# A two-block network on one core: routing rearranged, and the last layer's first expert group selected by TensorE

## The reference

```python
mix = jnp.concatenate([o_dn, o_sa.astype(o_dn.dtype)], axis=-1) @ w_out[l]
h = layer_norm(DEEPNORM_ALPHA * h + mix, ln1_g[l], ln1_b[l])
ffn = hier_moe(h, w_grp[l], b_grp[l], w_rtr[l], b_rtr[l], w1[l], w3[l], w2[l])
h = layer_norm(DEEPNORM_ALPHA * h + ffn, ln2_g[l], ln2_b[l])
...
    grp_prob = jax.nn.softmax((t @ w_grp).astype(F32) + b_grp, axis=-1)
    g_prob, g_sel = lax.top_k(grp_prob, 1)
...
    e_prob, e_sel = lax.top_k(jax.nn.softmax(in_grp, axis=-1), TOP_K_IN_GROUP)
...
    hid = jax.nn.silu(jnp.einsum('td,edf->tef', t, w1)) * jnp.einsum('td,edf->tef', t, w3)
    y = jnp.einsum('tef,efd->td', hid * combine[..., None].astype(hid.dtype), w2)
```

## Time and profile before

| | us |
|---|---|
| three executions | 1302.36, 1304.57, 1306.28 (median 1304.57) |
| profiled execution, its own time | 1303.69 |
| its span, first to last instruction | 1301.9 |
| TensorE busy | 1261.1 (97%) |
| VectorE / ScalarE / GpSimd busy | 573.9 / 485.3 / 115.3 |
| read from HBM | 301.06 MB |

### The profile page before, as it was taken

The page is one execution under the profiler, slowest core; times in us unless marked ns, Lnnn a source line. Parts: engine busy times, 40 slices in busy tenths (PEclk is TensorE's granted clock), DMA queues, the critical chain, the costliest instruction groups (busy, mean ns, idle before and its releaser), DMA issues.

```text
span 1301.9 us, 19435 instructions
## 1 busy us (share of the span) xinstructions
PE 1261.1 (97%) x7553; PEld 811.2 (62%) x7553; DVE 573.9 (44%) x1280; ACT 485.3 (37%) x1064; POOL 115.3 (9%) x167
## 2 busy tenths in 40 slices
PE   8999999999999999999999998999999989999996
PEld 7888588885787877554444433778877544344432
DVE  3335223262676585462222225677585443222224
ACT  3346343462753245212223233663235313223232
POOL 0000000000014321000000000004322000000000
PEclk9999999999999999999999999999999999999999
DMA  9753162332521124759999999221133769999994
GB/s 367 151 179 108 54 269 97 130 106 77 211 98 67 66 97 166 286 219 394 420 420 422 421 415 385 104 98 66 66 130 119 317 237 397 421 421 422 422 421 177
DMA packets 48847, 307.40 MB, mean 236 GB/s; under 512 B 5897, under 2 KB 6409, under 8 KB 16752
## 3 DMA queue, kind: packets, MB, share of 16 engines
q1 hardware_dynamic: 43760, 288.61, 56.3%
q0 software_dynamic: 3200, 8.16, 2.8%
q10 hardware_dynamic: 1792, 9.32, 1.9%
HBM read 301.06 MB, written 8.59 MB: 238 GB/s over the span
## 4 chain that ended last, share of the span: by engine, by line
PE 79%; DVE 13%; ACT 5%; issue 2%; DMA 1%; ACTq 0%; DVEq 0%; SPq 0%; POOLq 0%
PE ps L1151 22%; PE ps L1878 18%; PE ps L1905 9%; PE ps L1191 4%; PE ps L1455 4%; PE ps L1947 2%; PE ps L1968 2%; PE ps L1119 2%; DVE projT L2829 1%; DVE small L2828 1%; PE ps L1693 1%; PE ps L1887 1%; PE ps L1929 1%; DVE projT L2820 1%; PE ps L1584 1%
## 5 line engine op out<-in xcount | busy, mean ns | idle before, releaser
L1151 PE MATMUL ps<-hT,ring 128*128 128x272 f32 (+1 forms) x1760 | 416.8, 390 | 0.6 <-ACT hT L2065 0.6
L1151 PEld LDWEIGHTS ps<-hT,ring 128*128 128x128 f32 x1760 | 327.1, 190 | 62.7 <-issue 7.7
L1878 PE MATMUL ps<-ring,arena 128*64 128x512 f32 x416 | 138.6, 598 | 0.0
L3273 DVE TENSOR_TENSOR xo<-ps,xo 128x512 fp32r<-128x512 f32 x64 | 42.9, 689 | 99.6 <-ACT xo L2502 99.4
L3394 POOL TENSOR_TENSOR arena<-projT,cst 32x272 f32<-32x272 f32 x104 | 71.5, 688 | 114.2 <-DVE projT L2807 101.1
L1878 PE MATMUL ps<-projT,arena 128*64 128x512 f32 x240 | 80.0, 597 | 0.9 <-issue 0.9
L3264 DVE TENSOR_TENSOR arena<-arena,ps 128x256 f32<-128x256 f32 x32 | 13.5, 421 | 141.4 <-ACT arena L2489 140.8
L1878 PEld LDWEIGHTS ps<-ring,arena 128*64 128x64 f32 x416 | 40.2, 137 | 51.9 <-issue 51.1
L2487 ACT ACTIVATE arena<-ps 128x256 f32<-128x256 f32 x32 | 12.3, 383 | 138.0 <-PE ps L1878 138.0
L1455 PE MATMUL ps<-ring,projT 128*128 128x512 f32 x128 | 57.0, 598 | 0.0
L1191 PE MATMUL ps<-ring,arena 128*128 128x512 f32 x128 | 55.9, 593 | 0.0
(11 more groups left out here) (526 smaller groups left out, 2056.9 us busy)
## 6 DMA issues: line engine op xcount, KB each, us to landing
ring<-experts SPq DMA_DIRECT2D x72, 1024.0 KB, 16.5
ring<-w_in SPq DMA_DIRECT2D x62, 1024.0 KB, 5.6
projT<-experts SPq DMA_DIRECT2D x48, 1024.0 KB, 15.9
arena<-experts SPq DMA_DIRECT2D x22, 1024.0 KB, 12.6
prm<-experts SPq DMA_DIRECT2D x22, 1024.0 KB, 16.0
ring<-w_out SPq DMA_DIRECT2D x16, 1024.0 KB, 5.0
spare<-experts SPq DMA_DIRECT2D x12, 1024.0 KB, 14.6
lent<-experts SPq DMA_DIRECT2D x8, 1024.0 KB, 10.2
```

The lines of the kernel that those rows point to most:

```text
L1151: mm = pe.matmul(ps[:, chunk_bank(blk, l, j), 0:ncols], w[:, j % 2, k, :], hT[:, k, T - ncols:T], start=(k == 0), stop=(k == KC - 1))
L1878: mm = pe.matmul(ps[64 * e:64 * e + 64, 0, :], xg[:, 4 * h + k, i % 2, 64 * e:64 * e + 64], w[e][:, k // 2, 512 * (k % 2):512 * (k % 2) + ...
L3273: v.tensor_tensor(low, ps[:, 4 + half, :], high, ALU.subtract).then_inc(s("pair_rows_copied"), 1)
```

## The change

In both layers: tile 0's logits use 16 stationary columns and bank 0 (`logits_of`) in place of 128 columns and a copy; every tile's logits raise `logits_done`, and VectorE takes the tiles one by one; the four operations behind ScalarE's exponentials move behind the first pair selection; two fillers grow. In the last layer: `router_turn` and the logits of tile 1 move one step back in the out projection; TensorE selects the first group's rows itself from `res`, in two halves (`first_rows`); ScalarE copies them into `xrows`; the row numbers come later, from the places; GpSimd, SP, TensorE, VectorE and ScalarE no longer use a fetch for group 0. The stores of the normed rows stay, since groups 1 to 3 are still fetched.

```diff
+        def fetched(l, g):
+            return 16 * (GROUPS * l + g + 1 - (l == LAYERS - 1))
...
                         sp.wait_ge(layer_normed, normed_at[l, 1, 2, 1])
-                        sp.wait_ge(rows_fetched, 16 * (GROUPS * l + 1))
+                        if l < LAYERS - 1:
+                            sp.wait_ge(rows_fetched, fetched(l, 0))
...
+        def logits_of(t):
+            return ps[0:ROWS[t], 1 if t else 0, 64 * t:64 * t + 36]
...
-                        mm = pe.matmul(ps[:, 1, 64 * t:64 * t + 36], h2T[:, k, COL[t]:COL[t] + P], wr[:, k, :],
+                        mm = pe.matmul(logits_of(t), h2T[:, k, COL[t]:COL[t] + ROWS[t]], wr[:, k, :],
                                        start=(k == 0), stop=(k == KC - 1))
-                    if t != 1 or l == LAYERS - 1:
-                        mm.then_inc(s("logits_done"), 1)
+                    mm.then_inc(s("logits_done"), 1)
...
-                    if t == (0 if l < LAYERS - 1 else 2):
+                    if t == 0:
                         router_turn(0, 1)
...
                         if t == 2 and i == 0:
                             if l < LAYERS - 1:
                                 router_turn(1, 0)
-                            router_sums_made()
-                            router_logits(0, 1)
-                        if t == 2 and i == 1 and l < LAYERS - 1:
-                            router_logits(1, 0)
+                                router_sums_made()
+                                router_logits(0, 1)
+                            else:
+                                router_turn(0, 1)
+                        if t == 2 and i == 1:
+                            if l < LAYERS - 1:
+                                router_logits(1, 0)
+                            else:
+                                router_sums_made()
+                                router_logits(0, 1)
...
+                def first_rows(half):
+                    pe.wait_ge(s("group_selected"), 1)
+                    for t in tiles:
+                        mm = pe.matmul(ps[:, 2 + half, :], xsel[:, t, :], res[:, t, 512 * half:512 * half + 512],
+                                       start=(t == t0), stop=(t == 2))
+                    mm.then_inc(s("group_rows_done"), 1)
...
-                first_tokens()
-                keep_busy(5, 512, 512)
+                if l < LAYERS - 1:
+                    first_tokens()
+                    keep_busy(5, 512, 512)
+                else:
+                    first_rows(0)
                 pe.wait_ge(s("experts_chosen"), 2)
                 count_experts([2])
-                keep_busy(5, 256)
+                if l < LAYERS - 1:
+                    keep_busy(5, 384)
+                else:
+                    first_rows(1)
...
                     for k in range(KC):
+                        if i == 0 and l == LAYERS - 1 and k % 4 == 0:
+                            pe.wait_ge(s("group_rows_copied"), k // 4 + 1)
...
                 turn_group(0)
-                keep_busy(4, 448)
+                keep_busy(4, 448, 448)
...
+                    if l == LAYERS - 1:
+                        for half in range(2):
+                            a.wait_ge(s("group_rows_done"), half + 1)
+                            L(a.activation(xrows[:, 512 * half:512 * half + 512], ps[:, 2 + half, :], ACT.Copy),
+                              s("group_rows_copied"))
...
-                V(v.memset(xrows, 0.0))
+                if l < LAYERS - 1:
+                    V(v.memset(xrows, 0.0))
+                if l < LAYERS - 1:
+                    V(v.memset(lg[:, 0, 0:36], 0.0))
...
-                for t in tiles[:-1]:
+                for p, t in enumerate(norm_order(l)[:-1]):
+                    v.wait_ge(s("logits_done"), p + 1)
                     adjusted(t)
...
-                V(v.tensor_tensor(lg[:, 2, 388:392], ps[:, 1, 288:292], whole(group_marks)[:, 2, :], ALU.add))
-                V(v.tensor_reduce(mx[:, 1:2], lg[:, 2, 388:392], AX, ALU.max))
-                v.wait_ge(s("choice_exps_ready"), 1)
-                V(v.tensor_reduce(lg[:, t0:, 45], c(40, 4), AX, ALU.add))
-                V(v.tensor_scalar(c(100, 1), c(99, 1), 1.0, None, ALU.add))
-                V(v.tensor_tensor(c(100, 1), c(100, 1), c(45, 1), ALU.mult))
-                V(v.reciprocal(c(100, 1), c(100, 1)))
                 v.wait_ge(s("places_counted"), 2)
...
                   s("routing_ready"))
+                V(v.tensor_tensor(lg[:, 2, 388:392], ps[:, 1, 288:292], whole(group_marks)[:, 2, :], ALU.add))
+                V(v.tensor_reduce(mx[:, 1:2], lg[:, 2, 388:392], AX, ALU.max))
...
-                VP = Linked(v, s("pair_vec_order"))
+                VP = V
...
+                    if l == LAYERS - 1:
+                        v.wait_ge(s("pairs_selected"), 3)
+                        VP(v.tensor_reduce(mx[:, 0:1], xplaces[:, 2 * PER_GROUP:3 * PER_GROUP], AX, ALU.add))
+                        VP(v.tensor_scalar(group_tokens[:, 0:1], mx[:, 0:1], -0.5, float(NO_ROW - T // 2), ALU.mult, ALU.add),
+                           s("group_tokens_ready"))
...
                 select_pairs(0)
+                v.wait_ge(s("choice_exps_ready"), 1)
+                V(v.tensor_reduce(lg[:, t0:, 45], c(40, 4), AX, ALU.add))
+                V(v.tensor_scalar(c(100, 1), c(99, 1), 1.0, None, ALU.add))
+                V(v.tensor_tensor(c(100, 1), c(100, 1), c(45, 1), ALU.mult))
+                V(v.reciprocal(c(100, 1), c(100, 1)))
...
-                for group in range(GROUPS):
+                g.wait_ge(rows_stored, 16 * (3 * l + len(tiles_of(l))))
+                for group in range(l == LAYERS - 1, GROUPS):
                     g.wait_ge(s("group_tokens_ready"), group + 1)
-                    if group == 0:
-                        g.wait_ge(rows_stored, 16 * (3 * l + len(tiles_of(l))))
-                    if GROUPS * l + group:
-                        g.wait_ge(rows_fetched, 16 * (GROUPS * l + group))
+                    if l == LAYERS - 1 and group == 1:
+                        g.wait_ge(s("rows_split"), 1)
+                    if fetched(l, group - 1):
+                        g.wait_ge(rows_fetched, fetched(l, group - 1))
```

More of the change, by code:

```diff
@@ L530, in program @@
                  "pair_hidden_ready", "pair_hidden_turned", "pair_hidden_copied", "pair_down_done",
-                 "pair_rows_copied", "pair_summed", "router_vec_ready", "pair_vec_order",
+                 "pair_rows_copied", "pair_summed", "router_vec_ready", "group_rows_copied",
                  "group_sums_copied", "experts_back", "group_tokens_ready",
@@ L1923, in gather_pair @@
                     pe.wait_ge(s("pairs_selected"), selected(0, q))
-                    if i == 0:
-                        pe.wait_ge(rows_fetched, 16 * (GROUPS * l + 1))
-                    else:
+                    if i:
                         pe.wait_ge(s("pair_tokens_copied"), copies_of(i - 1))
+                    elif l < LAYERS - 1:
+                        pe.wait_ge(rows_fetched, fetched(l, 0))
                     for k in range(KC):
+                        if i == 0 and l == LAYERS - 1 and k % 4 == 0:
+                            pe.wait_ge(s("group_rows_copied"), k // 4 + 1)
                         mm = pe.matmul(ps[:, 2 + k // 4, (k % 4) * P:(k % 4 + 1) * P], xrows[:, k * P:(k + 1) * P],
@@ L2453, in experts_all @@
                         a.wait_ge(s("all_copied"), 1)
-                        a.wait_ge(rows_fetched, 16 * (GROUPS * l + 1))
+                        if l < LAYERS - 1:
+                            a.wait_ge(rows_fetched, fetched(l, 0))
                         a.dma_start(comb_dram, combT[0:EXPERTS]).then_inc(s("all_stored"), 16)
@@ L3042, in adjusted @@
                     v.wait_ge(deviation_ready, mean_at[l, 1, t])
-                    if n < P:
-                        V(v.tensor_copy(lg[:, t, 0:36], ps[:, 1, 64 * t:64 * t + 36]))
                     V(v.scalar_tensor_tensor(out=lg[0:n, t, 0:36], in0=router_sums[0:n, 0, :], scalar=lnm[0:n, t:t + 1],
-                                             in1=ps[0:n, 1, 64 * t:64 * t + 36], op0=ALU.mult, op1=ALU.add))
+                                             in1=logits_of(t), op0=ALU.mult, op1=ALU.add))
                     V(v.scalar_tensor_tensor(out=lg[0:n, t, 0:36], in0=lg[0:n, t, 0:36], scalar=rstd[0:n, t:t + 1],
@@ L3131, in _ @@
                 norm_centered(2, 1)
-                v.wait_ge(s("logits_done"), 2)
+                v.wait_ge(s("logits_done"), nt)
                 adjusted(2)
@@ L3139, in first_group_tokens @@
                 def first_group_tokens():
+                    if l == LAYERS - 1:
+                        return
                     v.wait_ge(s("group_rows_done"), 1)
@@ L3190, in experts_all @@
                     v.wait_ge(s("all_turned"), 1)
-                    v.wait_ge(rows_fetched, 16 * (GROUPS * l + 1))
+                    if l < LAYERS - 1:
```

(14 more changed lines are left out.)

## The result

| | before | after |
|---|---|---|
| median of 7 runs (range) | 1306.28 us (1302.36 to 1311.8) | 1297.3 us (1295.3 to 1301.35) |
| ratio of the runs, 95% interval | | 0.9946 (about 7 us), 0.9927 to 0.9964 |
| profiled execution (span) | 1303.69 (1301.9) | 1297.66 (1295.9) |
| mean granted clock of it | 0.995 | 0.996 |

The time lies in the predicted range, 0.2 us from the predicted 1297.1. The trace shows that the sum came out through errors of opposite sign.

A forecast was written before the change was run, and what follows sets the result against it. It took both expert stages to end with the weight stream. Layer 0's 1.1 us plus the last layer's 6.0 made 7.1, giving 1297.1 us against the mean of 1304.2; range 1294.3 to 1300.6.

The forecast's parts named there:

- Bound of the stages: Both expert stages: they end when the weight stream ends, TensorE arriving 2.2 us early in the last layer, 0.1 in layer 0.
- The stream: Last layer's expert loads: the 15th to 17th leave 9.6 us earlier, the stream runs 6.0 us earlier and is soon full again.
- if layer 0 moves by its gather: Sign of being wrong: layer 0's stage shifts with its gather, where the forecast had its end 1.1 us earlier.
- The other sign: Sign of being wrong: the last stage's end moves by no more than the start of its gather.
- Clock: Last layer's gather and first half of the first pair: they run at 2.4 GHz, worth 1.7 us more.
- Rival B: Last layer's first gather: the clock falls there all the same, 5.5 us gained in all, 1298.7 us; chance 12%.
- Part 1: Last layer's out projection: tile 1's transposes and logits move one step, filling a TensorE wait; 1.66 us, between 0 and 1.68.
- Part 2: Layer 0's small logits: 16 stationary columns in place of 128 for the meta rows; 1.1 us, bounds 0 and 1.2.
- Part 3: Last layer's first group: TensorE selects the rows without a fetch; gather starts at 1060.45 in place of 1063.13, 2.7 us.
- C: Last layer's stream: not refilled after the early loads, each slot's load paying 5.0 us on an empty queue; 1299.8 us, chance 10%.
- D: Layer 0's small logits: the 16-column product alone gains nothing; 6.0 us in all, 1298.2; chance 66% together with the forecast.
- E: Branch into the grouped code at both gathers: it becomes long after the edit, making the kernel slower, 1308.7 us; chance 4%.

The follow-up runs named there:

- e1: Kernel after, with SP's 15th load of the last layer also waiting for the first half of the first gather; median 1300.8 us, 1.0 +- 0.5 slower at equal clock.
- e4: Kernel after with the last layer's store and fetch of the first group kept; median 1301.56 us, +1.2 +- 0.5 at equal clock.
- e9: The kernel of e4 with more filler before both first gathers; median 1299.6 us, +1.0 +- 0.5 at equal clock against the kernel after.
- e2: Kernel after with four more 512-column filler products before layer 0's first gather; median 1301.22 us, 2.2 +- 0.5 slower at equal clock.
- e5: Kernel after with tile 1's transposes and logits in the last layer's out projection moved one step earlier again; median 1299.53 us, +1.9 +- 0.5 at equal clock.
- e11: Kernel before with only layer 0's 16-column logits and a memset for the copy; median 1305.28 us, -1.3 +- 0.4 at equal clock.
- e10: Kernel after, unchanged, timed again; median 1300.39 us over 12 runs, -3.8 +- 0.4 at equal clock against the kernel before.

## Why the prediction was right, point by point

- **Bound of the stages: wrong.** "Both expert stages end when the stream of weights ends", with TensorE there "2.2 us early in the last layer", took an end wait of 2 us for the sign of what sets the end. The 414 GB/s of the earlier trace rows is a mean over 216 us and hides the stage's first 25, where slots pace the loads: from 1063 to 1066 the engines are nearly empty, and from 1075 to 1090 they move 14% less than later. The failed step is the one worked out under "The stream": 9.6 us of earlier loads and a stream that "is full again soon". It gave 1.6 us beyond TensorE's own gain; the runs show 0.15 in the trace, and by e1 1.0 +- 0.5 for the early loads, which e4 and e9 do not confirm. The wait before pair 14's down projection, predicted below 1 us, stayed at 1.30, and the sum of the two end waits at 2.07 (2.19 before).
- **Layer 0: wrong by the same error, with the other sign.** TensorE's earlier start was priced at nothing. The full clock at its gather was worth 1.58 us to the end of the stage, and e2 shows a later start passed on in full. This is one of the prediction's own two signs of being wrong, "if layer 0 moves by its gather": its first freed slot came 2.74 us earlier and its end 2.85, and TensorE did not wait for weights there. The other sign did not show, as the last stage's end moved by more than the gather's start (6.05 and 4.23), but the difference is the clock's 1.67.
- **Clock: the size right, its nature missed.** 1.7 us at the last gather, 1.67 seen. But it was read as a fixed property of that place. In the traces three falls entered the sum, -1.6, -1.7 and +1.5; over runs the clock is worth 1.7 us in the mean. Rival B's test, whether the clock falls at that gather, can't be decided by one trace.
- **Part 1** 1.66: measured 1.88 (e5), above the stated bound of 1.68, which was an idle time and not a distance from start to start. **Part 2** 1.1: 1.0 (e11). **Part 3**'s start of the gather, 2.7 with part 1: 2.86; its own share of 0.8 to 0.9 is what e4 and e9 give.
- **Rivals.** C came closest in mechanism: the stream was not filled again by the early loads and the slots set it. Its reason, 5 us on an empty queue for each slot, was not what happened, and its price missed what layer 0 gained. D did not happen: the small product gained its 1.0. Nor did E, nor a fetch left somewhere.

The clock in layer 1 (+1.50) and the stream (+1.45) cost what layer 0's clock gave (-1.58) and more: the sum of -6.0 for -7.1 in the trace. That the median agreed to 0.2 us is luck, as e10's median of 1300.39 for the same kernel shows.

## What to carry to other kernels

- Before calling a stream the bound, cut its rate into short stretches from its start, and the busy share too, which alone did not show the dip here. If it is not full in the first of them, buffers set the pace, and an earlier start of the loads is worth little; what frees the first buffers is worth its full amount.
- A wait at a stage's end tells which resource arrives last, not which one's change would move it: here both moved together.
- Idle time in a trace of pipelined products is less than what removing it gives: 1.68 us of it was worth 1.88, and 0.92 was worth 1.19.
- Look where the clock falls in several traces before pricing it; compare kernels at equal mean clock. That brought the 95% interval from +- 2 to 4 us to about +- 0.8 and made a part of 1 us visible.

## What was not expected of the hardware

- Runs of one program, the kernel before, differ by 12 us (1300 to 1312), most of it granted clock (0.986 to 0.996, 1.01 us for each 0.001, with 1.2 us left over).
- The clock can stay at the 1.2 GHz level while TensorE's work is listed as gapless: in layer 0's routing of e2 it did so for 13.7 us with PE busy all the time. Before it fell, from 559.0 to 562.4, TensorE was busy for 2.83 of 3.40 us; in the kernel after it was busy for 2.90 in the same stretch, and the clock did not fall.
```profile
562.70:576.40 13.70, 13.70 (x30) 7.09 (x30) 6.87 (x26) 0.91 (x4) 1.09 (x1) 0.51 0.14 54
```
- A single core reads weights at 420 GB/s for 160 us while TensorE never pauses. The Trainium skill (Perfetto Trace Analysis, Roofline) has one core alone go beyond the 358 GB/s that the prediction cited; the trace agrees with that note and not with 358 as a limit.
